# Short bursts of unread TensorE products inside the norms of a two-block transformer kernel

## The chip, the cores and the metric

The kernel runs on one core of a Trainium2 chip. A core has a matrix engine (TensorE, PE in the profile, with its weight loads as PEld), a vector engine (DVE), a scalar engine (ACT), a GpSimd engine (POOL) and DMA queues that the engines issue to. The metric is the time in microseconds (us) that one execution takes on the device. Everything is computed in float32.

## The reference

Two blocks of two layers each work on 512 tokens of width 1024; the first block carries 256 context tokens beside them, so that its token axis has up to 768 columns. Each layer is a mixer (attention, or in the second block convolution, dilated attention and a gated scan) and a feed-forward part. In front of both stands a norm with a modulation, and one last norm ends the program:

```python
def _rms_norm(x, g):
    xf = x.astype(jnp.float32)
    y = xf * lax.rsqrt(jnp.mean(xf * xf, axis=-1, keepdims=True) + EPS)
    return (y * g.astype(jnp.float32)).astype(x.dtype)

def _modulate(x, g, shift, scale):
    return _rms_norm(x, g) * (1 + scale) + shift
...
        ax = _modulate(hx, norm1_g[i], sx1, cx1)        # before the mixer
        hx = hx + gx1 * yx
        hx = hx + gx2 * _mlp(_modulate(hx, norm2_g[i], sx2, cx2), mlp_w1[i], mlp_w2[i])
...
    return _rms_norm(hx, final_g)                       # ends each block
```

The norm at the end of the first block and the first one of the second follow each other without work between them; the kernel makes both in one stage (the double norm).

## The kernel before, in words

Activations lie transposed: the feature axis is cut into 8 blocks (KT = 8) of 128 partitions, the tokens are columns. X holds the residual, H the normed and modulated activations. The program is a list of phases, and every engine walks through it in the same order, with semaphores between the engines. There is no scheduler: the order on each engine is the order of the code.

A norm phase stands between two stretches of matrix products, and goes as follows (nt is the number of token tiles of 128, 6 or 4).

1. While the phase before still runs, ACT squares the finished blocks of X (`square`, L1370) and POOL adds six of the eight into ACC (L2358). The last two blocks stay apart in SQ.
2. PE sums over the partitions with products that have a single column: the tile of squares is the stationary operand and a column of ones is the moving one. ACC comes first (L961), then the last two blocks (L981), each behind its `sq_ready`. In the double norm there are further ones for the second set of squares (L967, L973). The last one tells ACT (`stats_ready`).
3. ACT takes the square root (L1472, after a table load and a dummy root at L1470), DVE the reciprocal (L1928). PE waits for `stats_inv`.
4. PE spreads the reciprocal roots over the partitions by transposes (L987, L990) into the two PSUM banks of slot 3, and tells DVE (`rstd_spread`).
5. DVE scales X block by block into H (L1956), ACT adds the shift (L1484) and counts `h_ready`. PE waits for the first block, and starts the next phase's products.

The next phase is either a plain product (kind "linear", L608: one group of 8 blocks, each 512 columns wide, in the first group behind one `h_ready` each), or a quick one (kind "quick"): feed-forward products by a scheme that saves multiplications with sums of weights and of tokens. There the first pass (L1136, L1148) goes block by block behind `h_ready`, and the third product set (L1116) waits for sums of tokens that DVE makes from all of H (L1972, L1975).

A float32 product of the program is two MATMUL instructions in the trace, each with its weight load; a transpose is one.

Of the kernel before, what the change touches and what calls it, by code (L numbers as in the profile page):

```python
# [231 lines left out]
def build(nc, a, out):  # L232
    PHASES, CHUNKS = plan()
    with ExitStack() as ctx:
        def sb(name, shape, dt=F32):
            return ctx.enter_context(nc.sbuf_tensor(name, shape, dt))
# [4 lines left out]
        ps = ctx.enter_context(nc.psum_tensor("ps", [P, 8, 512], F32))  # L241
# [25 lines left out]
        ones = sb("ones", [P, P])  # L267
        ones4 = sb("ones4", [P, P])
        ident = sb("ident", [P, P])
# [283 lines left out]
        def value_items(layer):  # L553

            its = ATT[layer]
            return its if layer != 1 else its[::2]
# [67 lines left out]
        def phase_index(kind, layer, nth=0):  # L624
            return [i for i, ph in enumerate(PHASES) if ph["kind"] == kind and ph["layer"] == layer][nth]

        first0 = phase_index("norm", 0)
# [170 lines left out]
        def buffers(layer):  # L798
            return (PB, PT, YT) if layer < 2 else (PB2, PT2, YT2)
# [5 lines left out]
        def s_slot(i):  # L805
            return psf[:, (i % 2) * 1024:(i % 2) * 1024 + 1024]
# [56 lines left out]

        @block.tensor
        def _(pe):
            def attention(layer):
                its, vals = ATT[layer], value_items(layer)
                base, vbase, p2, ybase = att_base[layer], val_base[layer], pt2_base[layer], yt_base[layer]
                pb, pt, yt = buffers(layer)
                per = 2 if layer == 1 else 1  # L870
                seconds = [sum(key_tiles(v) > 4 for v in vals[:j + 1]) for j in range(len(vals))]

                def scores(i):
                    q, ks, _ = pieces(layer, its[i])
                    if i >= 2:

                        pe.wait_ge(probs_ready, base + i - 1)
                    for k, off_ in ks:
                        n = 1
                        for d in k.shape[1:]:  # L880
                            n *= d
                        mm = nc.tensor.matmul(s_slot(i)[:, off_:off_ + n], q, k, start=True, stop=True)  # L882
                    mm.then_inc(scores_ready, 1)

                def turn(j):

                    nt = key_tiles(vals[j])
                    if layer == 1:

                        pe.wait_ge(probs_mixed, j + 1)  # L890
                    else:
                        pe.wait_ge(probs_ready, base + j + 1)
                    if j >= 1:

                        pe.wait_ge(pt_copied_act, vbase + j)
                        if seconds[j - 1]:
                            pe.wait_ge(pt_copied_dve, p2 + seconds[j - 1])
                    for t in range(nt):
                        src = pb[:, 2 * (j % 2) if layer == 1 else j % 2, t * P:(t + 1) * P]
                        mm = nc.tensor.transpose(ps[:, PT_BANK[t // 4], (t % 4) * P:(t % 4 + 1) * P], src, ident[:, :])  # L900
                    mm.then_inc(pt_ready, 1)

                def values(j):
                    nt = key_tiles(vals[j])
                    vt = pieces(layer, vals[j] if layer != 1 else vals[j])[2]

                    pe.wait_ge(pt_copied_act, vbase + j + 1)
                    if nt > 4:
                        pe.wait_ge(pt_copied_dve, p2 + seconds[j])
                    if j >= 1:  # L910

                        pe.wait_ge(y_ready, vbase + j)
                    for t in range(nt):
                        mm = nc.tensor.matmul(ps[:, O_BANK, (j % 2) * P:(j % 2 + 1) * P], pt[:, j % 2, t * P:(t + 1) * P],  # L914
                                              vt[t], start=t == 0, stop=t == nt - 1)
                    mm.then_inc(o_ready, 1)

                def turn_y(y):

                    pe.wait_ge(y_ready, vbase + (y + 1) * (1 if layer == 1 else 2))  # L920
                    if y >= 1:

                        pe.wait_ge(yt_taken, ybase + y)
                    nc.tensor.transpose(ps[:, Y_BANK, (y % 2) * P:(y % 2 + 1) * P], yt[:, y % 2, :], ident[:, :]).then_inc(yt_ready, 1)

                nv = len(vals)
                ys = {(2 * y + 1 if per == 1 else y): y for y in range(nv if per == 2 else nv // 2)}
                if layer >= 2:
                    conv_mean(layer - 2)
                for j in range(nv + 2 + per):  # L930
                    if layer >= 2 and j == 2:
                        conv_variance(layer - 2)
                    if j < nv:
                        for i in range(per * j, per * j + per):
                            scores(i)
                    if 2 <= j <= nv + 1:
                        values(j - 2)
                    if j >= 2 + per and j - 2 - per in ys:
                        turn_y(ys[j - 2 - per])
                    if 1 <= j <= nv:  # L940
                        turn(j - 1)

            def norm(i, g, cols):
                n = norm_phases.index(i)
                slot = psf[:, g.slot * 1024:(g.slot + 1) * 1024]
                nt = cols // P
                if g.turn:

                    pe.wait_ge(group_freed[g.slot], g.turn)

                if i == first0:
                    for j in range(KT - 1):

                        pe.wait_ge(sq_ready, j + 1)
                        for t in range(nt):
                            nc.tensor.matmul(slot[:, t:t + 1], H[:, j, t * P:(t + 1) * P], ones[:, 0:1], start=j == 0 and t == 0,
                                             stop=False, skip_group_check=True)
                else:
                    pe.wait_ge(sq_summed, (KT - 3) * n)
                for t in range(nt if i != first0 else 0):  # L960
                    nc.tensor.matmul(slot[:, t:t + 1], ACC[:, t * P:(t + 1) * P], ones[:, 0:1], start=t == 0, stop=False,  # L961
                                     skip_group_check=True)
                if i == double:

                    pe.wait_ge(sqg_summed, KT - 3)
                    for t in range(nt):
                        nc.tensor.matmul(slot[:, 8 + t:9 + t], ACCG[:, t * P:(t + 1) * P], ones[:, 0:1], start=False, stop=False,  # L967
                                         skip_group_check=True)
                    for j in range(KT - 2, KT):

                        pe.wait_ge(sqg_ready, j + 1)
                        for t in range(nt):
                            nc.tensor.matmul(slot[:, 8 + t:9 + t], SQG[:, j % 2, t * P:(t + 1) * P], ones[:, 0:1], start=False,  # L973
                                             stop=j == KT - 1, skip_group_check=True)

                for j in range(KT - 1 if i == first0 else KT - 2, KT):

                    pe.wait_ge(sq_ready, KT * n + j + 1)
                    last = H[:, j, :] if i == first0 else SQ[:, j % 2, :]
                    for t in range(nt):  # L980
                        mm = nc.tensor.matmul(slot[:, t:t + 1], last[:, t * P:(t + 1) * P], ones[:, 0:1], start=False, stop=j == KT - 1,  # L981
                                              skip_group_check=True)
                mm.then_inc(stats_ready, 1)

                pe.wait_ge(stats_inv, n + 1)
                for t in range(nt):
                    mm = nc.tensor.transpose(slot[:, t * P:(t + 1) * P], roots[:, 1, t:t + 1].broadcast_to([P, P]), ident[:, :])  # L987
                if i == double:
                    for t in range(nt):
                        mm = nc.tensor.transpose(slot[:, 512 + t * P:512 + (t + 1) * P], roots[:, 3, t:t + 1].broadcast_to([P, P]), ident[:, :])  # L990
                mm.then_inc(rstd_spread, 1)

            def together(groups):

# [215 lines left out]
            for i, ph in enumerate(PHASES):  # L1210
                kind, layer = ph["kind"], ph["layer"]
# [1440 lines left out]
```

## Time and profile before

| | |
|---|---|
| time, median of 3 runs | 3709.63 us (3707.96 to 3710.72) |
| the profiled execution | 3711.06 us |
| its span, first to last instruction | 3709.2 us |
| PE busy | 3544.0 us, 96% |
| DVE, ACT, POOL busy | 56%, 27%, 34% |
| mean granted TensorE clock | 0.972 |

The nine norms in order; the times are the start of the sums on PE in the profiled execution.

| norm | sums start, us | columns | next phase |
|---|---|---|---|
| 1 (first layer, start of the program) | 14.2 | 768 | linear |
| 2 | 467.95 | 768 | quick |
| 3 | 1061.86 | 768 | linear |
| 4 | 1524.01 | 512 | quick |
| 5 (double) | 1921.39 | 512 | linear |
| 6 | 2404.11 | 512 | quick |
| 7 | 2813.26 | 512 | linear |
| 8 | 3288.24 | 512 | quick |
| 9 (final) | 3697.15 | 512 | none, output |

A row of the timeline gives start, length, engine, line, what is written and read, shape and count, and in brackets how long the engine sat idle before it and who released it. A row of the stages gives the busy time of each engine in a stretch, with the number of instructions in brackets, and then PEclk, the clock that TensorE was granted as a share of full speed: 1.00 is 2.4 GHz, 0.50 is 1.2 GHz.

### The profile page before, as it was taken

To read this page: it belongs to the slowest core of one execution; us is meant where nothing else is said; L and a number is where in the kernel's file an instruction comes from. 1 tells how busy PE (TensorE), PEld (TensorE's weight loads), DVE (VectorE), ACT (ScalarE), POOL (GpSimd) and SP (SyncE) were. 2 spreads that over 40 slices of the span, in tenths; PEclk is the share of its full clock that TensorE was granted. 3 is DMA by queue.
4 is the path that set the end of the run, shared out by engine and by line. 5 is a ranking of instruction groups with operands and counts; after the bars stand their busy time and mean duration, and the time that the engine had idled before them with its cause. 6 is when DMAs were issued, how large, how long until landed. Compare 5 with 4: busy or idle time off the path is not lost. (4 is left out here: it accounts for less than half of the span.)

```text
span 3709.2 us, 43720 instructions
## 1 busy us (share of the span) xinstructions
PE 3544.0 (96%) x15896; PEld 2614.8 (70%) x15896; DVE 2078.8 (56%) x3525; ACT 995.8 (27%) x2305; POOL 1255.9 (34%) x1207
## 2 busy tenths in 40 slices
PE   8899999999999998999999988899999998989999
PEld 5598555555555966888875556688885565668887
DVE  7775456544442176465655177478864448635654
ACT  2067221001020054211120164322212045422221
POOL 1000322222231033444440017456542005636554
PEclk9999999999999999999999998899999998899999
DMA  7400113333321100244442200134442210022222
GB/s 246 165 1 1 40 63 125 110 117 114 119 75 57 52 1 6 96 161 159 159 129 74 71 8 12 37 124 155 159 148 95 74 38 15 9 67 86 89 88 80
DMA packets 91091, 317.61 MB, mean 86 GB/s; under 512 B 10816, under 2 KB 13152, under 8 KB 90880
## 3 DMA queue, kind: packets, MB, share of 16 engines
q1 hardware_dynamic: 64224, 218.34, 18.2%
q10 hardware_dynamic: 24768, 90.19, 6.6%
q0 software_dynamic: 1888, 6.29, 0.6%
q8 instruction: 130, 2.13, 0.2%
q14 instruction: 81, 0.66, 0.1%
HBM read 312.68 MB, written 2.10 MB: 85 GB/s over the span
## 5 line engine op out<-in xcount | busy, mean ns | idle before, releaser
L1116 PE MATMUL ps<-arena 128*128 128x256 f32 (+1 forms) x3744 | 953.2, 408 | 3.7 <-DVE arena L1975 3.7
L1116 PEld LDWEIGHTS ps<-arena 128*128 128x128 f32 x3744 | 711.5, 190 | 209.7 <-issue 7.5
L608 PE MATMUL ps<-hbuf,ring 128*128 128x512 f32 (+1 forms) x1440 | 575.7, 562 | 7.6 <-ACT hbuf L1484 5.9
L608 PEld LDWEIGHTS ps<-hbuf,ring 128*128 128x128 f32 x1440 | 277.0, 193 | 302.4 <-issue 290.4
L2398 POOL TENSOR_TENSOR arena<-ring,arena 128x512 f32<-128x512 f32 (+1 forms) x140 | 182.6, 1304 | 844.5 <-PE ps L1116 844.5
L2381 POOL TENSOR_TENSOR arena<-ring 128x512 f32<-128x512 f32 (+1 forms) x140 | 179.8, 1284 | 440.3 <-DVEq L543 287.6
L1116 PE MATMUL ps<-arena,ring 128*128 128x256 f32 (+1 forms) x1104 | 292.5, 407 | 3.1 <-ACT arena L1414 3.1
L1890 DVE CUSTOM_DVE_ANT_0 aring<-aring,csil,adab 128x1024 f32<-128x1024 f32 x176 | 262.0, 1510 | 1.7
L1116 PEld LDWEIGHTS ps<-arena,ring 128*128 128x128 f32 x1104 | 209.3, 190 | 64.4 <-ACT arena L1414 5.9
L1994 DVE SCALAR_TENSOR_TENSOR resid<-ps,mod,resid 128x256 f32<-128x256 f32 (+2 forms) x296 | 137.6, 482 | 205.7 <-PE ps L1116 188.3
L914 PEld LDWEIGHTS ps<-arena 128*128 128x128 f32 x1440 | 176.7, 193 | 85.4 <-ACT arena L1309 61.1
L1994 DVE SCALAR_TENSOR_TENSOR resid<-arena,mod,resid 128x256 f32<-128x256 f32 (+1 forms) x168 | 109.2, 669 | 208.2 <-ACT arena L1414 205.0
L914 PE MATMUL ps<-arena 128*128 128x128 f32 x1440 | 206.0, 287 | 19.9 <-ACT arena L1323 12.5
L2392 POOL TENSOR_TENSOR arena<-ring 128x512 f32<-128x512 f32 (+1 forms) x140 | 219.8, 1570 | 0.0
L882 PE MATMUL ps<-arena 128*128 128x256 f32 (+2 forms) x656 | 205.0, 439 | 12.1 <-ACTq L543 9.0
L1414 ACT ACTIVATE arena<-ps 128x256 f32<-128x256 f32 (+1 forms) x140 | 57.5, 410 | 538.1 <-PE ps L1116 538.1
L2387 POOL TENSOR_TENSOR arena<-arena,ring 128x512 f32<-128x512 f32 (+1 forms) x140 | 190.0, 1357 | 19.2 <-issue 0.8
L1136 PE MATMUL ps<-hbuf,ring 128*128 128x256 f32 (+1 forms) x672 | 184.8, 420 | 8.5 <-ACT hbuf L1484 7.5
L619 PEld LDWEIGHTS ps<-ring,hbuf 128*128 128x128 f32 x1632 | 183.2, 192 | 2.0 <-issue 1.9
L619 PE MATMUL ps<-ring,hbuf 128*128 128x128 f32 x1632 | 183.2, 275 | 0.0
L1300 ACT ACTIVATE arena<-ps,small 128x512 f32<-128x512 f32 (+3 forms) x208 | 149.9, 722 | 109.1 <-DVE small L1795 109.0
L1148 PE MATMUL ps<-hbuf,ring 128*128 128x256 f32 (+1 forms) x672 | 178.6, 408 | 0.4
(276 smaller groups left out, 5096.6 us busy)
## 6 DMA issues: line engine op xcount, KB each, us to landing
aring<-in_ada ACTq DMA_DIRECT2D x172, 512.0 KB, 4.6
ring<-in_mlp SPq DMA_DIRECT2D x128, 512.0 KB, 3.8
ring<-in_up SPq DMA_DIRECT2D x88, 512.0 KB, 3.3
ring<-in_in SPq DMA_DIRECT2D x56, 512.0 KB, 3.2
ring<-in_down SPq DMA_DIRECT2D x32, 512.0 KB, 3.5
ring<-in_odd_in SPq DMA_DIRECT2D x24, 512.0 KB, 3.2
arena<-in_ada SPq DMA_DIRECT2D x16, 512.0 KB, 13.8
ring<-in_out SPq DMA_DIRECT2D x16, 512.0 KB, 3.2
```

The costliest lines, as they stand in the source:

```text
L608: mm = nc.tensor.matmul(slot[:, lo:hi], ring[:, c % RING, k, :], src[:, kt, lo:hi], start=kt == k0, stop=kt == k0 + nkt - 1)
L619: mm = nc.tensor.matmul(slot[:, t * P:(t + 1) * P], lhs[:, k], ring[:, c % RING, k, :], start=k == 0, stop=k == KT - 1)
L882: mm = nc.tensor.matmul(s_slot(i)[:, off_:off_ + n], q, k, start=True, stop=True)
L914: mm = nc.tensor.matmul(ps[:, O_BANK, (j % 2) * P:(j % 2 + 1) * P], pt[:, j % 2, t * P:(t + 1) * P], vt[t], start=t == 0, stop=t == nt - 1)
L1116: mm = nc.tensor.matmul(ps[:, bank, 0:tw], w, x, start=start and j == 0, stop=j == len(pairs) - 1, skip_group_check=True)
L1136: mm = nc.tensor.matmul(ps[:, XB[m % 2], 0:p.tw], f0[:, j], x[:, j, 0:p.tw], start=j == 0, stop=j == p.h - 1, skip_group_check=True)
L1890: nc.vector.tensor_tensor_reduce(wt, wt, csil[:, 0, :], 1.0, adab[:, layer, nb:nb + 1], ALU.mult, ALU.add, mod[:, layer, nb, 0:1]).then_in ...
L1994: x = nc.vector.scalar_tensor_tensor(out=X[:, blk, a_:b_], in0=src[:, a_ - lo:b_ - lo], scalar=mod[:, layer, p.gate + blk, s_:s_ + 1], in1 ...
L2381: nc.gpsimd.tensor_tensor(s[0], f1[:, 0:h], f1[:, h:2 * h], ALU.add).then_inc(wsum_ready, 1)
L2387: nc.gpsimd.tensor_tensor(s[1], s[0], f0[:, 0:h], ALU.subtract).then_inc(wsum_ready, 1)
L2392: nc.gpsimd.tensor_tensor(s[2], f0[:, 0:h], f1[:, 0:h], ALU.subtract).then_inc(wsum_ready, 1)
L2398: nc.gpsimd.tensor_tensor(s[3], f0[:, h:2 * h], s[1], ALU.subtract).then_inc(wsum_ready, 1)
```

## The change

PE gets a helper that issues n products of 128x128 by 128 columns from two constant tiles, the identity and the ones. They write to 128 columns of a PSUM bank, which no instruction reads before they are written anew. It is called in norms 2 to 9: three products before the last two squares, four after the sums have been handed to ACT, and, except in the final norm, five after the reciprocal roots are spread. Norm 1 stays as it was. Nothing else changes, on PE or elsewhere.

```diff
@@ -863,6 +863,11 @@
         @block.tensor
         def _(pe):
+            def keep_clock(bank, n):
+
+                for _ in range(n):
+                    nc.tensor.matmul(ps[:, bank, 384:512], ident[:, :], ones[:, :], start=True, stop=True, skip_group_check=True)
+
...
@@ -973,6 +978,8 @@
+                if i != first0:
+                    keep_clock(7, 3)
                 for j in range(KT - 1 if i == first0 else KT - 2, KT):
 
                     pe.wait_ge(sq_ready, KT * n + j + 1)
@@ -981,6 +988,8 @@
                         mm = nc.tensor.matmul(slot[:, t:t + 1], last[:, t * P:(t + 1) * P], ones[:, 0:1], start=False, stop=j == KT - 1,
                                               skip_group_check=True)
                 mm.then_inc(stats_ready, 1)
+                if i != first0:
+                    keep_clock(7, 4)
 
                 pe.wait_ge(stats_inv, n + 1)
                 for t in range(nt):
@@ -989,6 +998,8 @@
                     for t in range(nt):
                         mm = nc.tensor.transpose(slot[:, 512 + t * P:512 + (t + 1) * P], roots[:, 3, t:t + 1].broadcast_to([P, P]), ident[:, :])
                 mm.then_inc(rstd_spread, 1)
+                if i != first0 and PHASES[i]["kind"] != "final":
+                    keep_clock(5, 5)
```

PE's order in norm 6 before the change, a norm of 512 columns with a quick phase behind it (each row is a form with its count of products):

```order
L961 MATMUL ps<-ones,arena 128x1 x4
L981 MATMUL ps<-ones,arena 128x1 x8
L987 MATMUL ps<-ident,roots 128x128 x4
L1136 MATMUL ps<-hbuf,ring 128x256 x4
L1148 MATMUL ps<-hbuf,ring 128x256 x4
```

The same place with the change; L869 is the helper, and the lines behind it have moved down (L961 is now L966, L981 L988, L987 L996, L1136 L1147, L1148 L1159):

```order
L966 MATMUL ps<-ones,arena 128x1 x4
L869 MATMUL ps<-ones,ident 128x128 x3
L988 MATMUL ps<-ones,arena 128x1 x8
L869 MATMUL ps<-ones,ident 128x128 x4
L996 MATMUL ps<-ident,roots 128x128 x4
L869 MATMUL ps<-ones,ident 128x128 x5
L1147 MATMUL ps<-hbuf,ring 128x256 x4
L1159 MATMUL ps<-hbuf,ring 128x256 x4
```

The three, four and five products stand between rows that keep their order.

## Rows read from the trace of the kernel before

**Rows 1.** The page: granted clock in 40 slices of the span, in tenths.
```profile
PEclk9999999999999999999999998899999998899999
```
**Rows 2.** Waits of PE: who waited for whom, us in total, times, longest us.
```profile
PE ps L1136 <- ACT hbuf L1484: 7.5, 4, 2.5
...
PE ps L608 <- ACT hbuf L1484: 5.9, 3, 2.5
PE ps L987 <- DVE roots L1928: 5.3, 8, 0.7
```
**Rows 3.** Timeline of PE in norm 6.
```profile
2404.11 1.05 PE L961 MATMUL ps<-ones,arena 128*128 128x1 f32 x8 [0.84 <-DVE resid L1757]
2405.02 1.93 PE L981 MATMUL ps<-ones,arena 128*128 128x1 f32 x16
2407.58 0.65 PE L987 MATMUL ps<-ident,roots 128*128 128x128 f32 x4 [0.64 <-DVE roots L1928]
2409.92 3.75 PE L1136 MATMUL ps<-hbuf,ring 128*128 128x256 f32 x8 [1.69 <-ACT hbuf L1484]
2413.46 2.69 PE L1148 MATMUL ps<-hbuf,ring 128*128 128x256 f32 x8
2416.53 0.67 PE L1116 MATMUL ps<-arena 128*128 128x256 f32 x2 [0.37 <-DVE arena L1975]
```
**Rows 4.** Stages: busy us of PE, PEld, DVE, ACT, POOL; clock; DMA.
```profile
486.60:489.90 3.30, 3.30 (x6) 1.78 (x7) 3.30 (x3) 0.00 (x0) 0.00 (x0) 0.50 0.24 94
...
1066.90:1073.60 6.70, 4.22 (x10) 2.15 (x9) 5.62 (x11) 4.44 (x9) 0.00 (x0) 0.50 0.01 6
...
1927.00:1937.20 10.20, 6.94 (x14) 3.75 (x15) 7.46 (x16) 5.73 (x10) 0.00 (x0) 0.50 0.22 77
2404.90:2408.20 3.30, 2.66 (x23) 2.37 (x22) 0.18 (x1) 1.63 (x3) 1.82 (x2) 1.00 0.29 117
2408.30:2415.00 6.70, 5.08 (x12) 4.12 (x13) 6.53 (x11) 5.60 (x9) 0.00 (x0) 0.50 0.00 0
...
2817.90:2824.60 6.70, 5.53 (x7) 2.47 (x8) 5.37 (x11) 6.32 (x9) 0.21 (x1) 0.50 0.42 141
...
2188.00:2385.00 197.00, 164.63 (x881) 123.05 (x882) 129.93 (x239) 90.20 (x246) 119.78 (x195) 0.84 0.04 11
```
**Rows 5.** The page: products of 128 columns elsewhere in the program.
```profile
L619 PE MATMUL ps<-ring,hbuf 128*128 128x128 f32 x1632 | 183.2, 275 | 0.0
```
**Rows 6.** Timeline of ACT in norm 7.
```profile
2814.09 0.63 ACT L1370 ACTIVATE arena<-resid 128x512 f32<-128x512 f32 x1 [1.00 <-DVEq L2090]
2814.74 1.28 ACT L1470 ACT_TABLE_LOAD   x1
2816.04 0.20 ACT L1470 ACTIVATE roots<-small 128x1 f32<-128x1 f32 x1
2816.15 0.25 ACT L1472 ACTIVATE roots<-ps,small 128x4 f32<-128x4 f32 x1
```
**Rows 7.** Timeline of PE in norm 7.
```profile
2814.07 1.93 PE L981 MATMUL ps<-ones,arena 128*128 128x1 f32 x16
2816.73 0.65 PE L987 MATMUL ps<-ident,roots 128*128 128x128 f32 x4 [0.73 <-DVE roots L1928]
2819.07 6.46 PE L608 MATMUL ps<-hbuf,ring 128*128 128x512 f32 x8 [1.69 <-ACT hbuf L1484]
```
**Rows 8.** Timeline of PE in the double norm 5.
```profile
1928.57 1.12 PE L987 MATMUL ps<-ident,roots 128*128 128x128 f32 x4 [1.77 <-DVE roots L1936]
1929.48 1.06 PE L990 MATMUL ps<-ident,roots 128*128 128x128 f32 x4
1932.23 13.01 PE L608 MATMUL ps<-hbuf,ring 128*128 128x512 f32 x24 [1.69 <-ACT hbuf L1484]
```
**Rows 9.** Timeline of DVE in norm 6.
```profile
2408.27 5.36 DVE L1956 SCALAR_TENSOR_TENSOR hbuf<-resid,gs,ps 128x512 f32<-128x512 f32 x8 [0.74 <-PE ps L987]
```
**Rows 10.** Timeline of ACT in norm 3.
```profile
1069.16 8.47 ACT L1484 ACTIVATE hbuf<-hbuf,mod 128x512 f32<-128x512 f32 x16 [2.92 <-DVE hbuf L1956]
```

## The prediction, made before the changed kernel ran

> **What bounds the kernel now.** I read the page first: PE is busy for 96% of the span (the table of the profile), and its clock stands at 0.9 or less in a few slices only [rows 1]. So every microsecond that a norm takes on PE's path counts, and nothing else is near a bound. The waits of PE come next: it waits in the norms for the reciprocals (5.3 us over eight of them, 0.7 at most) and for the first modulated block (7.5 us before the quick phases, 5.9 before the linear ones, 2.5 at most each) [rows 2]. These are the holes that the change fills. Then the timeline of one norm: the single-column sums follow each other without a hole (1.05 us, then 1.93), a hole of 0.64, four transposes, a hole of 1.69, and the next phase's first pass [rows 3]. Last the clock by stages: in norm 6 it is 1.00 up to 2408.2, in which stretch PE was busy for 2.66 of 3.30 us, with single-column sums nearly all of it, and 0.50 from 2408.3 to 2415.0 [rows 4]. Norm 3 and norm 7 have 6.7 us at 1.2 GHz as well, the double norm 10.2, and norm 2 has a second fall of 3.3 us further on [rows 4].
>
> **What the clock costs now.** Only time in which PE is both slow and the one that is waited for. A 512-column product instruction at half clock takes about 0.85 us (8 in 6.46 us [rows 7]), twice what it takes at the full one.
> - Norm 7: PE starts the linear phase at 2819.07, is never idle again, and is slow until 2824.7 [rows 4, 7]: 5.6 us at half clock, so 2.8 lost. ACT hands over a block every 0.66 us there (DVE's pace, 5.36 us for 8 [rows 9]), quicker than PE's 2 x 0.43, so PE is the bound.
> - Norm 5: from 1932.23 to 1937.2, 5.0 us, so 2.5 lost [rows 4, 8].
> - Norm 2: the second fall, 3.3 us with PE busy throughout, 1.7 lost [rows 4].
> - Norm 3: with 768 columns ACT hands over a block every 1.06 us (8.47 us for 8 [rows 10]), slower than PE's 0.86. Two blocks at 1.7 instead of 1.06 put PE 1.3 behind, and the six others win back 0.2 each: 0.1 to 0.3 are left, I take 0.3.
> - Norms 4, 6 and 8: the first pass (4 + 4 products of 256 columns) is waited for by no one. PE ends it about 2416.15 and waits again until DVE has its token sums, at 2416.53 [rows 3]. Faster products there only lengthen this wait: 0.
> In all 7.3 us could come back at most. The scans lose far more (197 us at a mean of 0.84 in one of them [rows 4]), and the change does not touch them.
>
> **What the products cost.** The only rows of this form are the 1632 instructions of L619, 183.2 us busy, 0.112 us each at the full clock [rows 5]. At the half clock the nearest rows are the transposes of the double norm: from 1928.57 to 1929.48 for four, 0.23 each [rows 8]. A product is two instructions.
> - The burst of three (6 instructions, 0.67 us) stands before the last two squares. PE does not wait there: L981 starts the moment L961 has issued [rows 3]. In norm 7 the last square is done at 2814.09 + 0.63 = 2814.72, and PE needs it only half-way through its 1.93 us, at 2814.97 [rows 6, 7]. So it goes onto the path in full. What it could hide behind is ACT's table load and dummy root, which end at 2816.24, against PE's end of 2816.00; L1472 starts at 2816.15, so PE has 0.1 us to spare [rows 6, 7]. This holds for norms 4, 7 and 9; in norms 2, 3, 5, 6 and 8 the table is there earlier. Sum: 5 x 0.67 + 3 x 0.57 = 5.1 us.
> - The burst of four (8 instructions, 0.89 us) stands in the hole before the transposes. In norm 6 the sums' last issue ends about 2406.81 (0.14 before the modelled end 2406.95) and the transposes start at 2407.58, 0.77 later [rows 3]. The transposes queue behind the burst: 0.12 late. Seven norms: 0.8 us. In the double norm the hole is 1.77 [rows 8]: nothing. At the half clock it is 1.84 against 0.77, so 1.07 late, 0.95 more than at the full one. The first scaling on DVE waits for the transposes, ACT for DVE, and the next phase for ACT.
> - The burst of five (10 instructions, 1.12 us) lies in a hole of 1.69 or more, 1.85 from the transposes' last issue: hidden at the full clock. At the half one it is 2.3: 0.45 late, and in norms 4, 6 and 8 even this is caught up, because DVE sets the time there.
> So 5.9 us if all bursts run at the full clock, in a place where 7.3 can be won. The Trainium skill ("TensorE: Matmul & The Clock Gate", Back-to-back issue gap) gives about 81 ns for a 128-column product in a stream with weight loads. By that the three bursts would cost 0.49, 0.65 and 0.81 us, and the sum would be 5 x 0.49 + 3 x 0.39 = 3.6 instead of 5.9. The 0.112 us of rows 5 decides, since it is this kernel's own form.
>
> **How much clock comes back.** The bursts put full-width products among the single-column ones, but leave a stretch of them (L981, 1.93 us at 512 columns, 2.8 at 768) between burst three and four, and the longer one of the double norm ahead of burst three (L961, L967, L973). The trace shows that the clock fell behind just such a stretch in norm 6 [rows 4]. I expect it to hold in about two of three norms with 512 columns, and to fall in most with 768 and in the double one. Where it falls, bursts four and five then leave PE with hardly a hole, so it should rise sooner than now. Norm 7: 0.8 x 2.8 = 2.2. Norm 5: half of 2.5, 1.3. Norm 2: half of 1.7, 0.8. Norm 3: 0.1. Together 4.4 us back. Against this stands burst four at the half clock in a third of seven norms: 0.95 x 7 / 3 = 2.2.
> Sum: +5.9 - 4.4 + 2.2 = +3.7 us. Against the profiled execution's 3711.06 (span 3709.2 and 1.9 around it) that is 3714.8, and against the median of 3709.63 it is 3713.3; the profiled execution lies 1.4 above the median, and I predict the median: 3713.
>
> **The rivals.**
> - The clock holds everywhere. All 7.3 comes back and no burst is slow: 5.9 - 7.3 = -1.4, so 3708.2. For it: the holes are what the bursts fill. Against it: the fall came while PE was busy. The Trainium skill (same page, HAM oscillation) puts the loss of clock down to gaps in which PE idles. By that rule the single-column sums would be no danger and this rival would be the likely one; the row of 2404.9 to 2408.2, 2.66 us busy in 3.30 and then the fall, does not fit it well.
> - The bursts are hidden and the clock comes back, because PE's issue has room that the trace does not show and burst three costs nothing. Then 0.8 + 0 - 7.3 = -6.5 at best, 3703.1. The nearest rows, 0.112 us per instruction without any hole, speak against it.
> - Slower than before by more: the clock falls ahead of burst four, in the stretch of L981, which burst three has moved later. Its place is the transposes' wait, its price 1.07 instead of 0.12 in each norm; it decides as soon as this happens in about half of the norms. In all seven, and with the double norm unchanged: 5.9 + 7 x 0.95 + 2 x 0.45 = 13.5, less 2 to 3 for an earlier rise in norms 5 and 7, so +11, 3720.5.
> - The change does not do what it says: the falls stay where they are, and only the cost is left, +5.9 to +8: 3716.5.
>
> **Chances and range.** Forecast 0.50 (3713, its own range 3710 to 3716.5), clock held everywhere 0.17, hidden bursts 0.05, slow bursts 0.12, no effect on the clock 0.16. What a measurement of this kernel can tell from no change is about 0.2%, 7.4 us: below 3702.2 or above 3717.0. Faster than that needs more than the most that the norms lose, 0.04. Slower needs the slow bursts, or no effect with a little more, 0.14. The rest, 0.82, is the same. The bounds of the unknown terms (clock back 0 to 7.3, slow bursts 0 to 6.7) give 3708 to 3722; I leave out the far ends and take 3706.5 to 3719, with the lower end widened for the runs' own spread of 2.8 us.
>
> **What the next profile would show.** The helper's 91 products (8 x 3, 8 x 4, 7 x 5) of two instructions at about 0.112 us each; L981's first instruction 0.67 us after L961's last; L1472 0.57 to 0.67 later after the first sum than now; the transposes 0.1 behind the fourth product, in norms where the clock is 1.00; the hole before L1136 and L608 down to 0.6. In norms 5 and 7 the stage at 0.50 after the first L608 should shrink from 5.0 and 5.6 us. I am wrong if PE turns out to have waited at L981, if the clock stays at 1.00 through all norms, or if norms 4, 6 and 8 get shorter, which would mean that DVE was not their bound.

## The result, and the profile after

The changed kernel takes 3717.8 us in the median of 20 runs, the kernel before 3709.9 in as many: a ratio of 1.0024, with a 95% interval of 1.0018 to 1.0030, so 7.9 us or 0.24% slower. The forecast was 3713 with a range of 3706.5 to 3719: the sign is right, the rise of 3.7 us that was forecast is half of the 7.9 that came. The profiled execution took 3716.7 us, 5.7 more than that of before, and its mean granted clock is 0.977 instead of 0.972. So the clock did come back, and the time went up all the same. Of all executions compared in this document one was not in the fast state (of the experiment full_sums_holes, 5180.5 us at a mean clock of 0.668), and it is left out.

The page shows the same picture as before at this scale; PE is 18 us busier.

```profile
span 3714.9 us, 44084 instructions
...
PE 3562.4 (96%) x16078; PEld 2633.8 (71%) x16078; DVE 2076.2 (56%) x3525; ACT 996.9 (27%) x2305; POOL 1258.5 (34%) x1207
```

Timeline of PE in norm 6, which answers to [rows 3]. This is the place where the clock stayed full.

```profile
2405.41 1.05 PE L966 MATMUL ps<-ones,arena 128*128 128x1 f32 x8 [0.84 <-DVE resid L1768]
2406.32 0.91 PE L869 MATMUL ps<-ones,ident 128*128 128x128 f32 x6
2407.07 1.84 PE L988 MATMUL ps<-ones,arena 128*128 128x1 f32 x16
2408.78 1.14 PE L869 MATMUL ps<-ones,ident 128*128 128x128 f32 x8
2409.75 0.60 PE L996 MATMUL ps<-ident,roots 128*128 128x128 f32 x4
2410.19 1.28 PE L869 MATMUL ps<-ones,ident 128*128 128x128 f32 x10
2412.04 2.58 PE L1147 MATMUL ps<-hbuf,ring 128*128 128x256 f32 x8 [0.57 <-ACT hbuf L1495]
2414.58 2.67 PE L1159 MATMUL ps<-hbuf,ring 128*128 128x256 f32 x8
2418.64 1.53 PE L1127 MATMUL ps<-arena 128*128 128x256 f32 x6 [1.39 <-DVE arena L1986]
```

From the first sum to the first transpose it is 4.34 us now (2409.75 - 2405.41), and was 3.47: 0.87 more, with 0.79 forecast. The first pass starts 0.8 late, runs at full speed (2.58 us where it took 3.75), and then PE waits 1.39 us for DVE instead of 0.37. The faster products bought nothing here, as the prediction has it.

Timeline of PE in the double norm 5, which answers to [rows 8].

```profile
1921.75 0.95 PE L966 MATMUL ps<-ones,arena 128*128 128x1 f32 x8
1922.56 1.03 PE L972 MATMUL ps<-ones,arena 128*128 128x1 f32 x8
1923.46 2.25 PE L978 MATMUL ps<-ones,arena 128*128 128x1 f32 x16
1925.56 1.63 PE L869 MATMUL ps<-ones,ident 128*128 128x128 f32 x6
1926.98 3.41 PE L988 MATMUL ps<-ones,arena 128*128 128x1 f32 x16
1930.26 2.06 PE L869 MATMUL ps<-ones,ident 128*128 128x128 f32 x8
1932.16 1.12 PE L996 MATMUL ps<-ident,roots 128*128 128x128 f32 x4
```

Here the clock fell already in L978, at 1924.9, near its end. The burst of three costs 1.4 us instead of 0.67, and the same 16 instructions of L988 that took 1.84 us in norm 6 take 3.41. The transposes come 10.41 us after the first sum, where it was 7.18.

Timeline of PE in norm 7, which answers to [rows 7]. The clock falls inside the burst of four; the rest of that burst, the transposes and the burst of five are slow (the four transposes take 1.06 us, the burst 2.12), and the linear phase starts with the full clock.

```profile
2815.38 0.95 PE L966 MATMUL ps<-ones,arena 128*128 128x1 f32 x8
...
2818.65 1.56 PE L869 MATMUL ps<-ones,ident 128*128 128x128 f32 x8
2820.00 1.06 PE L996 MATMUL ps<-ident,roots 128*128 128x128 f32 x4
2820.86 2.12 PE L869 MATMUL ps<-ones,ident 128*128 128x128 f32 x10
2822.81 4.47 PE L608 MATMUL ps<-hbuf,ring 128*128 128x512 f32 x10
```

The stages, which answer to [rows 4]: norm 2 with its fall now ahead of the sums' end, the stretch behind it, which held the second fall of before, norm 3 and norm 6 without any fall, norms 5 and 7, and norm 9.

```profile
470.90:477.60 6.70, 6.70 (x32) 6.70 (x33) 1.80 (x4) 0.71 (x2) 1.63 (x2) 0.50 0.00 0
477.70:500.00 22.30, 19.12 (x54) 9.37 (x54) 17.14 (x23) 9.78 (x20) 3.75 (x3) 1.00 0.07 24
1063.90:1075.00 11.10, 9.74 (x59) 6.68 (x58) 6.69 (x14) 5.79 (x14) 1.76 (x4) 1.00 0.18 59
1921.80:1924.80 3.00, 3.00 (x30) 3.00 (x28) 0.82 (x3) 2.19 (x3) 1.94 (x4) 1.00 0.52 146
1925.00:1935.10 10.10, 10.10 (x48) 9.96 (x48) 1.77 (x7) 1.05 (x5) 1.69 (x4) 0.50 0.38 126
...
2405.50:2415.00 9.50, 8.93 (x62) 7.26 (x62) 4.95 (x9) 6.14 (x10) 2.52 (x3) 1.00 0.17 56
...
2819.20:2822.60 3.40, 3.40 (x19) 3.40 (x18) 1.66 (x4) 0.72 (x2) 1.05 (x2) 0.50 0.73 220
...
3703.30:3705.00 1.70, 1.70 (x9) 1.70 (x10) 0.18 (x1) 0.27 (x2) 0.00 (x0) 0.50 0.00 0
```

I then laid the two traces of PE beside each other, instruction by instruction, without the helper's. For each norm the table has how much later than before the next phase's first product starts, counted from the last product ahead of the sums, and how much of that is left 64 instructions further on (in norm 9, at the end of the program). The second profile is that of the experiment no_final below, which has the same bursts in norms 2 to 8.

| norm | late at the next product | left | left, second profile |
|---|---|---|---|
| 2 | +2.70 | +1.01 | +1.08 |
| 3 | +0.31 | 0.00 | +0.31 |
| 4 | +0.35 | +0.35 | +0.36 |
| 5 | +3.23 | +0.75 | +1.29 |
| 6 | +0.82 | +0.81 | +1.54 |
| 7 | +1.63 | -1.22 | +0.43 |
| 8 | +1.72 | +1.67 | +1.46 |
| 9 | +2.45 | +2.45 | (no bursts) |
| sum | +13.2 | +5.8 | +6.5 in 2 to 8 |

In all, 13.2 us late and 7.4 got back. The rest of the program adds -0.2 between these two traces. The clock falls in five of the eight norms, and these five make 11.7 of the 13.2 us: 2, 5 and 9, where it falls before the last sums are through, 2.4 to 3.2 us each, and 7 and 8, where it falls inside the burst of four, 1.6 and 1.7. The other three, 3, 4 and 6, make 1.5 together. In norms 2 to 8 the second profile has 6.5 us where the first has 3.4; with norm 9 that spans 5.8 to 8.9, and the measured 7.9 lies within.

### The profile page after: what moved, and what is told of

The parts are those of the page before. It is cut to its first block and busy times, and to the rows that moved or that the text cites. A ratio compares the mean times of both kernels' runs of the same rounds, so it can differ in the third digit from the quotient of the medians.

```text
span 3714.9 us, 44084 instructions
## 1 busy us (share of the span) xinstructions
PE 3562.4 (96%) x16078; PEld 2633.8 (71%) x16078; DVE 2076.2 (56%) x3525; ACT 996.9 (27%) x2305; POOL 1258.5 (34%) x1207
## 3 DMA queue, kind: packets, MB, share of 16 engines
q0 software_dynamic: 1888, 6.29, 0.6%
## 5 line engine op out<-in xcount | busy, mean ns | idle before, releaser
L608 PE MATMUL ps<-hbuf,ring 128*128 128x512 f32 (+1 forms) x1440 | 570.1, 558 | 3.2 <-DVEq L543 1.8
L608 PEld LDWEIGHTS ps<-hbuf,ring 128*128 128x128 f32 x1440 | 273.8, 191 | 295.0 <-issue 279.3
L1147 PE MATMUL ps<-hbuf,ring 128*128 128x256 f32 (+1 forms) x672 | 179.6, 408 | 2.9 <-ACT hbuf L1495 1.6
L1159 PE MATMUL ps<-hbuf,ring 128*128 128x256 f32 (+1 forms) x672 | 180.2, 409 | 0.6
```

Of the source, the lines that this page charges most:

```text
L608: mm = nc.tensor.matmul(slot[:, lo:hi], ring[:, c % RING, k, :], src[:, kt, lo:hi], start=kt == k0, stop=kt == k0 + nkt - 1)
L1147: mm = nc.tensor.matmul(ps[:, XB[m % 2], 0:p.tw], f0[:, j], x[:, j, 0:p.tw], start=j == 0, stop=j == p.h - 1, skip_group_check=True)
L1159: mm = nc.tensor.matmul(ps[:, WB, 0:p.tw], f0[:, p.h + j], x[:, p.h + j, 0:p.tw], start=j == 0, stop=j == p.h - 1, skip_group_check=True)
```

## The experiments

The experiments were timed in five rounds, each beside the kernel before on the same chip. The changed kernel's row is that of the section above, and before_again, at the end, is a single execution. Kernels of different sets are compared by their ratios to the kernel before. "Mean clock" is the granted clock averaged over the executions of a kernel; for the kernel before it is 0.972 to 0.973 in these sets, which is 202 to 206 us at half clock.

| kernel | ratio to before (95%) | mean clock |
|---|---|---|
| changed kernel | 1.0024 (1.0018 to 1.0030) | 0.977 |
| three_only | 1.0009 (1.0001 to 1.0018) | 0.973 |
| four_only | 1.0001 (0.9992 to 1.0010) | 0.975 |
| five_only | 1.0003 (0.9994 to 1.0011) | 0.975 |
| five_again | 1.0007 (0.9998 to 1.0015) | 0.974 |
| one_column | 1.0039 (1.0026 to 1.0052) | 0.971 |
| no_three | 0.9989 (0.9980 to 0.9997) | 0.979 |
| no_final | 1.0022 (1.0013 to 1.0031) | 0.976 |
| two_norms | 0.9997 (0.9988 to 1.0006) | 0.975 |
| holes_only | 0.9984 (0.9976 to 0.9993) | 0.978 |
| full_sums | 0.9976 (0.9967 to 0.9984) | 0.980 |
| full_sums_holes | 0.9972 (0.9961 to 0.9984) | 0.983 |

My theory was that a burst costs its issue time wherever PE is the one waited for, that this is set against the clock it brings back in the norms before a linear phase, and that a burst which runs at half clock costs double. The first rival was that the slow bursts in the waits make nearly all of the loss. The second was that the activity of the products does nothing and only their number counts.

**One burst at a time.** The changed kernel with two of its three calls removed:

```diff
-                if i != first0:
-                    keep_clock(7, 3)
...
-                if i != first0:
-                    keep_clock(7, 4)
```

(This is five_only; three_only and four_only keep the first or the second call instead.)

three_only: 

> Only the burst of three (norms 2 to 9) is kept. Path theory (each burst costs its issue time where PE is the one waited for, and the clock that comes back in norms 5 and 7 is set against it): 5 x 0.67 + 3 x 0.57 = 5.1 us on the path and nearly no clock back, since the last sums of single columns and both waits still lie behind it, so +5 to +6 us, mean clock as before (0.972). Slow-burst theory (most of the changed kernel's +7.9 comes from bursts that run at 1.2 GHz in the waits): +5, since this burst comes before the fall. If PE has spare issue time there: below +2.

Measured 3714.6 us against 3711.1, +3.4, with an interval of +0.4 to +6.7. That is less than the +5 to +6 that I expected, though the interval holds both, and the clock is as before. Its profiled execution was the slowest of its eleven (3725.1 us), so its trace says little about this median.

four_only: 

> Only the burst of four, behind the handover of the sums, is kept. Path theory: the transposes of the changed kernel came 0.20 us later after the root than before where the clock was full, so 7 x 0.2 = +1.4 us at the full clock, and 0.9 to 1.0 more in each norm in which the clock falls before the burst has ended; the clock should rise sooner in norm 5. Together +1 to +4. Slow-burst theory: +5 or more, nearly the whole of the change. No effect: within 1 us.

Measured +0.4 us (-3.0 to +3.7). Not the loss of 5 or more that the first rival asks for, and a little better than my range.

five_only: 

> Only the burst of five, behind the transposes, is kept. Path theory: it lies in a hole of 1.7 us or more, costs nothing at the full clock and up to 0.45 us at the half one, and brings the clock back earlier in norms 5 and 7 (in the changed kernel norm 7 was 1.2 us shorter over all): -1 to -3 us, mean clock 0.974 or more. If bursts bring no clock back by themselves: 0 to +1 us and 0.972.

Measured +1.1 us (-2.2 to +4.1) at a mean clock of 0.975. The clock rose as I expected, the time did not fall. Norm by norm its profile agrees with the theory: norm 5 is 1.64 us shorter, norm 7 1.70, all eight together 3.5. In its clock record the falls of norms 2 to 8 begin where they did before, to 0.2 us, and last 3.4 us instead of 6.8 (6.8 instead of 10.2 in norm 5). What it lost is elsewhere; see the scans below. The three alone add up to +4.9 us, the three together cost 7.9: the difference of 3 us is no larger than the intervals, but see no_three.

**The same products with a single column.**

```diff
-                    nc.tensor.matmul(ps[:, bank, 384:512], ident[:, :], ones[:, :], start=True, stop=True, skip_group_check=True)
+                    nc.tensor.matmul(ps[:, bank, 384:385], ident[:, :], ones[:, 0:1], start=True, stop=True, skip_group_check=True)
```

> All three bursts stay in place, but each product has a single moving column instead of 128: the issue of an instruction stays (0.112 us, as for the sums), its activity goes. Path theory: the whole path cost of 5.1 + 1.4 = 6.5 us, nothing back, and slow bursts in every norm in which the clock falls in the longer single-column stretch, so +8 to +12 us, slower than the changed kernel by 1 to 4, clock 0.971 or below. If the products' activity changes nothing: the same time as the changed kernel, +7.9. If the changed kernel's loss came from the columns themselves rather than from the issue: below +3.

Measured 3726.6 us against 3711.1: +14.5 by the ratio (+9.6 to +19.3), above my range of 8 to 12 but the right way, with the lowest clock of all. Its interval overlaps a little with that of the changed kernel (+6.7 to +11.1), but each of its five executions (3723.3 to 3730.1) took as long as the slowest of the changed kernel's twenty (3723.3) or longer. Timeline of PE in norm 7 of this kernel, and the stages there:

```profile
2820.34 0.95 PE L966 MATMUL ps<-ones,arena 128*128 128x1 f32 x8
2821.15 0.81 PE L869 MATMUL ps<-ones,ident 128*128 128x1 f32 x6
2821.82 2.13 PE L988 MATMUL ps<-ones,arena 128*128 128x1 f32 x16
2823.82 1.84 PE L869 MATMUL ps<-ones,ident 128*128 128x1 f32 x8
2825.52 1.09 PE L996 MATMUL ps<-ident,roots 128*128 128x128 f32 x4
2826.41 2.13 PE L869 MATMUL ps<-ones,ident 128*128 128x1 f32 x10
2828.40 4.62 PE L608 MATMUL ps<-hbuf,ring 128*128 128x512 f32 x5
...
2820.40:2823.30 2.90, 2.90 (x29) 2.90 (x27) 0.65 (x2) 2.10 (x3) 1.85 (x4) 1.00 0.64 194
2823.40:2833.50 10.10, 10.10 (x32) 7.17 (x32) 6.03 (x12) 6.25 (x10) 1.81 (x4) 0.50 0.38 129
```

The bursts take as long as with 128 columns (0.11 us an instruction at the full clock, 0.21 at the half one), and PE has no idle time in these rows. Nevertheless the clock is 0.50 from 2823.4 to 2833.5, and L608 starts in it: 5 instructions in 4.62 us. The two kernels issue the same instructions and differ in the columns of each alone; with 128 the mean clock is 0.977, with one 0.971. So for the clock it was the columns that made the difference here and not the number of instructions, and the second rival falls. The changed kernel's columns gave back some 7 us (14.5 less 7.9) of the cost that its instructions make.

**Taking away what stands on the path.** The edits of no_three (the first call goes), no_final (the condition of the first and second call) and two_norms (the condition of all three) on the changed kernel:

```diff
# no_three
-                if i != first0:
-                    keep_clock(7, 3)
# no_final, also at keep_clock(7, 4)
-                if i != first0:
+                if i != first0 and PHASES[i]["kind"] != "final":
                     keep_clock(7, 3)
# two_norms, also at the other two calls
-                if i != first0:
+                if i in (norm_phases[4], norm_phases[6]):
                     keep_clock(7, 3)
```

no_three: 

> The changed kernel without its burst of three: four and five products in norms 2 to 8, four in norm 9. Path theory: the burst of three is the one that stands where PE does not wait, so its removal takes away most of the +8 us: between -4 and +1 us against before. If the three bursts only cost in proportion to their number (12 products a norm, +8): +6.

Measured 3707.3 against 3710.4 us, ratio 0.9989: -4.1 (-7.4 to -1.1). The burst of three is the harmful one: without it the kernel is faster than the one before. Its share of the +7.9 is 12 us (each of the two figures has some 3 us either way), more than its issue time of 5.1. In the two profiles, which are 12.0 us apart, the eight norms make 8.8 of it (+5.8 against -3.0 by the measure of the table) and the two stretches described at the end of this section 2.7. One way to cost more than its issue is this: standing ahead of the last sums, the burst moves these and the burst of four later, to where the clock is low. In the double norm of no_three, L986 (the last sums) takes 1.93 us instead of 3.41:

```profile
1923.28 1.93 PE L978 MATMUL ps<-ones,arena 128*128 128x1 f32 x16
1925.07 1.93 PE L986 MATMUL ps<-ones,arena 128*128 128x1 f32 x16
1926.85 1.79 PE L869 MATMUL ps<-ones,ident 128*128 128x128 f32 x8
1928.76 1.11 PE L994 MATMUL ps<-ident,roots 128*128 128x128 f32 x4
```

This pair alone doesn't show it, for where the fall lands differs from execution to execution. The experiment holes_only has no burst ahead of these sums either, and in its profile they are slow all the same:

```profile
1923.68 3.55 PE L986 MATMUL ps<-ones,arena 128*128 128x1 f32 x16
1927.10 1.63 PE L869 MATMUL ps<-ones,ident 128*128 128x128 f32 x6
```

So the harm of this burst is measured; how its 12 us divide into issue time, slow sums and luck is open.

no_final: 

> The changed kernel without bursts in norm 9, behind which there is no product that a faster clock could help. Path theory: 0.8 us less than the changed kernel at the full clock and up to 2.4 less in an execution in which the clock falls before its burst of four, so +5.5 to +7.5 us against before. If norm 9 doesn't matter: +8.

Measured +8.2 us (+4.8 to +11.5). It can't be told from the changed kernel; the 0.8 to 2.4 us that norm 9 costs in the timeline are too small for this comparison.

two_norms: 

> The changed kernel's three bursts, but only in the norms 5 and 7, behind which a linear phase starts that PE bounds. Path theory: their own cost of 0.67 to 0.87 each and 2 to 4 us of clock back: -2 to 0 us, at a mean clock of 0.973 to 0.974; the +8 of the changed kernel is then made in the six other norms. If the cost lies in the bursts wherever they are: +2.

Measured -1.1 us (-4.5 to +2.2): the loss is gone, so it is made in the six other norms, as the theory has it. Whether something is won in norms 5 and 7 the interval leaves open.

**Only the holes.** The first call goes, the second has three products, and norm 9 has none:

```diff
-                if i != first0:
-                    keep_clock(7, 3)
...
-                if i != first0:
-                    keep_clock(7, 4)
+                if i != first0 and PHASES[i]["kind"] != "final":
+                    keep_clock(7, 3)
```

> The burst in front of the last squares is gone, the second has three products (0.67 us, less than its hole of 0.77), the third five, and the final norm has none. Path theory: no product stands on the path at the full clock, and the clock comes back in norms 3, 5 and 7 as with the burst of five alone: between -4 and 0 us, mean clock 0.975 to 0.977. If bursts have a cost that the norms' timelines don't show (the burst of five alone measured +1 us although its eight norms were 3.5 us shorter in the profile): 0 to +3 us at the same clock.

Measured 3702.0 us against 3709.8, ratio 0.9984: -5.9 (-8.9 to -2.6), more than expected. Eight products a norm instead of twelve, none of them where PE is waited for at the full clock, and the clock of the changed kernel or better.

**Sums with full-width activity.** If the columns make the difference and a single-column product takes the same 0.112 us as one of 128 columns, the sums themselves can carry the activity, with not one instruction more. This starts from the kernel before, without a burst (in its double norm L967 and L973 likewise, into the second bank):

```diff
-                    nc.tensor.matmul(slot[:, t:t + 1], ACC[:, t * P:(t + 1) * P], ones[:, 0:1], start=t == 0, stop=False,
+                    nc.tensor.matmul(slot[:, t * P:(t + 1) * P], ACC[:, t * P:(t + 1) * P], ones[:, :], start=t % 4 == 0, stop=False,
...
-                nc.scalar.activation(roots[:, 0, 0:nt], slot[:, 0:nt], ACT.Sqrt, bias=small[:, 40:41]).then_inc(stats_root, 1)
+                nc.scalar.activation(roots[:, 0, 0:nt], slot[:, 0:nt] if i == first0 else slot[:, 0:nt * P:P], ACT.Sqrt, bias=small[:, 40:41]).then_inc(stats_root, 1)
```

> The kernel before without any burst; in norms 2 to 9 the sums of squares have 128 moving columns of ones instead of one, so that each result stands 128 times, and ACT and DVE read every 128th column. As many instructions, and by the path theory the same time for each (0.112 us, which the weight load of 128 columns sets, as in the 128-column products elsewhere), but full-width activity where the clock now falls. Path theory: the clock holds through the sums and falls later and for less time, 30 us or more fewer at the half clock, mean 0.976 to 0.978, and -4 to -9 us. If it is the holes and not the single-column sums that cost the clock: within 1 us of before, 0.972. If a 128-column product is dearer than a single-column one: +1 or more.

Measured 3699.8 us against 3709.8, ratio 0.9976: -8.9 (-12.2 to -5.9), at the upper end of what I expected. Timeline of PE in its double norm and at the linear phase behind it:

```profile
1919.54 1.05 PE L961 MATMUL ps<-ones,arena 128*128 128x128 f32 x8
1920.43 1.06 PE L967 MATMUL ps<-ones,arena 128*128 128x128 f32 x8
1921.32 1.95 PE L973 MATMUL ps<-ones,arena 128*128 128x128 f32 x16
1923.11 1.95 PE L982 MATMUL ps<-ones,arena 128*128 128x128 f32 x16
1926.83 0.65 PE L988 MATMUL ps<-ident,roots 128*128 128x128 f32 x4 [1.77 <-DVE roots L1937]
```

The 16 instructions of L982 take 1.95 us; with a single column they took 1.93. The clock is full up to the transposes (0.65 us for four, 1.12 before [rows 8]). Over norms 2 to 8 the falls of this profile begin 7.1 to 9.5 us after the first sum, where those of before begin 3.6 to 5.6 us after it, and norm 7 has none. Together with unread bursts in the two holes alone (three products, then five):

> The sums with 128 moving columns, and unread bursts in the two holes alone (three products, then five; none in the final norm). Path theory: the clock holds in nearly all of norms 2 to 8, 50 us or more fewer at the half clock, mean 0.979 to 0.981, and -7 to -11 us against before. If bursts have a hidden cost: 1 to 4 us slower than the full-width sums alone.

Measured 3698.9 us, ratio 0.9972: -10.4 (-14.5 to -5.9). It can't be told from full_sums, though the clock is higher still, 0.983. In its profile the clock falls in none of norms 2 to 9; in its double norm the stage from the sums to the next phase's first products is

```profile
1918.60:1930.00 11.40, 9.73 (x76) 8.69 (x75) 4.62 (x13) 5.48 (x11) 3.81 (x7) 1.00 0.47 153
```

These two are the fastest versions found, and both beat the kernel before and the changed one. In the profile of full_sums the eight norms account for 5.5 us of the gain and the two stretches of the next paragraph for 5.1.

**Where five_only lost its gain.** The two stretches from behind a linear phase's start to the next norm's sums, with attention and scan in them, have no line of the change. I had called them untouched. Stages of five_only, from norm 5 to norm 6 and from norm 7 to norm 8:

```profile
1960.30:2402.40 442.10, 402.34 (x1888) 264.19 (x1887) 240.58 (x427) 157.73 (x380) 135.35 (x208) 0.93 0.12 38
2847.40:3289.80 442.40, 403.88 (x1888) 264.63 (x1887) 239.97 (x427) 157.58 (x380) 135.71 (x208) 0.93 0.12 38
```

The same stretches of full_sums:

```profile
1958.50:2394.60 436.10, 398.95 (x1889) 261.30 (x1887) 239.55 (x427) 157.28 (x380) 135.19 (x208) 0.94 0.12 39
2838.60:3275.30 436.70, 396.91 (x1888) 261.20 (x1887) 240.53 (x427) 157.29 (x380) 135.16 (x208) 0.95 0.12 39
```

The instructions are the same to one or two, DVE's and ACT's busy time to 1 us, and still the pair takes 884.5 us in one kernel and 872.8 in the other. What differs is PE's busy time (806 against 796) and its clock. The kernel before has 877.8. To see whether this is chance I ran two kernels again, without any edit.

five_again: 

> The burst of five alone once more, since it measured +1.0 us in the mean (interval of the ratio 0.9994 to 1.0011) while its profile showed the eight norms 3.5 us shorter. If the burst is free and the first measurement was a draw of the scans' clock falls: -2 to -4 us. If it has a cost outside the norms' timelines: +1 again.

Measured +2.6 us (-0.7 to +5.6); the gain of 2 to 4 us that a free burst would have brought did not come. Its stretches take 442.1 and 441.3 us, where the first profile has 442.1 and 442.4.

before_again: 

> The kernel before, for a second profile. If the runs' spread comes from where in the scans the clock happens to fall, the stretches from norm to norm agree to 0.1 us but for the two with a scan, which may differ by several us, and the norms by up to 2 us each.

One execution, 3710.2 us. Its stages for the same two stretches:

```profile
1961.40:2401.80 440.40, 400.64 (x1888) 263.45 (x1887) 240.57 (x427) 157.67 (x380) 135.34 (x208) 0.93 0.12 38
2848.60:3286.00 437.40, 400.27 (x1889) 262.27 (x1887) 240.51 (x427) 157.46 (x380) 136.07 (x208) 0.94 0.12 38
```

They agree with the first profile of before (440.5 and 437.4 us) to 0.1, and so does each norm but norm 2, which is 1.25 us shorter. My expectation of several us of chance was wrong for this kernel. It isn't repeatable for every one: the changed kernel has 440.6 and 438.0 us, and no_final, the same up to there, 436.1 and 442.1. Over all fourteen profiles each stretch lies between 435.9 and 443.1 us. The time goes along with the clock record: of the two stretches 116 us are at half clock in the kernel before, 130 in five_only and 99 in full_sums, and between the two extremes of the fourteen (871.9 us in two_norms with 102 at half clock, 884.5 in five_only) 12.6 us more go with 27 us more at half clock. In five_only the stretches are 6.7 and 5.5 us longer in the two profiles, more than the 3.5 and 3.4 us that its norms gained.

So the clock in the scans makes a pair up to 7 us longer or 6 shorter than in the kernel before. That the bursts bring this about, by shifting where in the scans the clock falls, is likely from the two pairs of profiles that agree (five_only with five_again, before with before_again), but with two of each it is not shown; nor why a given shift makes a scan longer.

## Why the prediction was right, and where it was not

- **What bounds the kernel, and who can use the clock.** Right. The first passes of norms 4, 6 and 8 ran at full speed and PE waited longer for DVE (in norm 6 1.39 us after 0.37); norm 7 and norm 5 gave back 2.9 and 2.5 us between their first product and the 64th after it, norm 2 1.7.
- **The burst of three on the path.** Right in place and size at the full clock: in norm 4 the root starts 0.56 us later after the first sum, in norm 6 0.66. In all it is the burst that makes the change a loss (no_three).
- **The burst of four, 0.12 late.** It was 0.20 (0.87 in norm 6 with the burst of three, less its 0.67). Over seven norms 0.6 us too little.
- **The burst of five hidden.** Right at the full clock; at the half one it is 2.1 us, and PE goes on without a wait.
- **The clock that comes back: 4.4 us.** Too small: 7.4 in the profile, as much as the 7.3 that I had put as the most (norm 7 2.9, norm 5 2.5, norm 2 1.7, norm 3 0.3).
- **Bursts at half clock: 2.2 us.** This term was mis-sized most. I priced only the burst of four, in a third of seven norms. The delay at the next product sums to 13.2 us; 5.1 for the burst of three and 1.4 for that of four leave 6.7, three times the term. The clock fell in five norms of eight, and in three of them not behind the sums but within them. In norm 5 it fell near the end of L978, so that the burst of three, L988 and the burst of four ran at half speed; in norm 2, from 470.9 on, and in norm 9 it fell within L988, so that the rest of these sums and the burst of four were slow, in norm 9 with nothing to win. The rival "slow bursts" had this mechanism. Its price of 0.95 fits norms 7 and 8, about 0.9 each beyond the full-clock cost, but in norms 2, 5 and 9 it is 1.7 to 2.6 each (norms 3, 4 and 6 came 1.0 below theirs together, in part because the transposes of 3 and 4 were no longer slow). I gave it 0.12 and a count of norms that is too high for this trace: in norms 3, 4 and 6 the clock held.
- **Scans untouched.** Wrong, as shown; in the profiled pair it makes +0.8 us, so it does not explain that pair's difference, but it could have hidden or doubled a change of this size.
- **The rule on idle gaps.** The Trainium skill ("TensorE: Matmul & The Clock Gate", HAM oscillation) puts the loss of clock down to gaps of PE. This case shows it fall with PE busy all the time: 3.00 of 3.00 us in 1921.80 to 1924.80 with single-column sums, and the fall behind it. one_column shows the same with bursts, 2.90 of 2.90 us in 2820.40 to 2823.30. Busy here is what the rows count, each instruction from its start to its modelled end, with a single column moved in it.

The forecast of 3713 was 4.8 us low. The median lies outside the range that I gave to the forecast's own story (3710 to 3716.5) and 1.2 us inside the whole one. That it came this near is in part luck: the term of the slow bursts was 4.5 us too low and the clock that comes back 3.0 too low, and these work against each other. Taking the profile's terms instead of mine (+5.1 + 1.4 + 6.7 - 7.4) gives +5.8 for one execution, and the second profile's norms would give up to +8.9. The rival "no effect on the clock" came nearest in number (3716.5) and is wrong in its mechanism, for the mean clock rose from 0.972 to 0.977.

## What to carry to other kernels

Before filling a wait of TensorE, look whether it is one: products put where it is the engine that others wait for cost their issue time, and double once the clock is down. In this kernel it was the columns moved, and not the number of instructions, that kept the clock up, so first look for instructions that are already there and move few of them: widening them costs nothing where, as here, an instruction with one column takes as long as one with 128 (full_sums: -8.9 us without an instruction added, against +7.9 for 91 products more). And compare stretches that a change doesn't touch: here they differ by several us through the clock alone.

## What the runs showed of the hardware

- An instruction with one moving column and one with 128 take the same, 0.11 us, when each has its own 128-column weight load: 16 of them 1.93 and 1.95 us at the full clock; with one column 3.41 at the half one, and 8 with 128 columns 2.06.
- The same 1888 PE instructions take 436 to 443 us in the stretch with the scan, by where and for how long the clock falls. Two executions of the kernel before that started norm 2 0.45 us apart agreed to 0.1 us in every norm behind norm 2 and in both stretches with a scan.
- The time of a kernel and its mean clock are no measure of each other: at 0.977 the changed kernel is slower than the one before at 0.972.
